# u's rows ordered by step and chunk, turned by VectorE; state tables loaded by GpSimd, a block at a time

## The chip, the cores and the metric
The kernel runs on one core of a Trainium2 chip. The metric is the device time of one execution in microseconds, median of the runs.

## The reference
A trunk of two decoder layers on 256 tokens of width 2048, in float32. Layer 0 mixes tokens by a chunked gMLP unit, layer 1 by an S5 state space. Each layer then has a SwiGLU block (width 5632) and a gated per-layer embedding; a last RMS norm follows. The part that the change touches:

```
x = x + sigmoid(rms_norm(x) @ ple_w_gate[0]) * (p[0] @ ple_w_proj[0])   # stage gate0
u = rms_norm(x) @ w_in                                                   # stage win
bu = B_bar u            (128 groups of 16 channels, complex state of 64)
s[t] = lam_bar * s[t-1] + bu[t]                                          # scan over 256 tokens
y = Re(C s) + D u;  g = gelu(y);  val, gate = split(g @ w_out)           # stage out1
x = x + val * sigmoid(gate)
```

The recurrence is computed in 32 chunks of 8 steps: a table TQ takes a chunk's 8 steps of u to the increment of the state, a scan over 32 chunks gives the state at each chunk's start, TD takes it to the 8 outputs, and TK adds what the steps of a chunk give each other.

## The kernel before, in words
Every large product goes through one pipeline of 792 weight tiles (two blocks of 128 rows by 512 columns, 512 KB). SP loads tile t into RAW, ACT writes its rounded part WHI (L771), VectorE the rest WLO (L1049), and TensorE (PE) multiplies: 12 matmuls a tile (L1515 to L1517). The ring has four places, so ACT and VectorE run at most three tiles ahead of PE. `plan()` lists the tiles by stage: v, us, out0, up0a, dn0a, up0b, dn0b, gate0, win, out1 and so on; W0 is the first tile of win. Each engine has its list written out by hand: `until(t)` does that engine's part of the tiles up to t + 2, and what stands behind it is done between tiles, in order. A wait holds up everything behind it on that engine.

Operands are turned in two ways: the last four blocks of a stage by PE through `turn`, the others by a VectorE block transpose ZT, four stores to zd in DRAM (L485), and a load HT (L489); `high` (ACT) and `low` (VectorE) then write the operand's two parts, with a scale from VEC.

Tables. In the stages up0a to dn0b GpSimd computes, for each of 16 blocks, QT and DT; at BUILD_A PE transposes QT by eight 128x128 transposes (`turn_tables`, L1624) into two banks, ACT copies them to QS (L898), SP stores QS, DT and later EXP to tabq, tabd, tabk. At BUILD_B PE computes `taps` (L1633).

Use. In gate0 and win SP loads TQ, TE, TD, TK for a duo of two blocks at a time (a megabyte each but TE), between the weight loads. In win, column n of u is taken by ACT into Z (scaled by RC, the reciprocal of ROOT), turned by PE (`turn_u`, L1724), copied by VectorE with the steps in front (`u_chunks`, UC, L1404), stored to ud and loaded as UP by ACT's queue (`store_u`, `spread_u`, L950 and L958). PE does `into_states(d)` (L1739) for duos d = 2n and 2n + 1, VectorE `scan(d)` (L1414 to L1430), PE `out_of_states(d)` (L1757, L1765), ACT `take_y` (L966), VectorE `turn_y` (L1437), ACT `y_high` (L973), VectorE `y_low` (L1442). On PE turn_u and out_of_states use the same banks 6 and 7, so out_of_states waits for u_chunks of the column behind. The places are tile numbers in UT_AT, INTO_AT, OUT_AT, Y_AT.

Of the kernel before, what the change touches and what calls it, by code (L numbers as in the profile page):

```python
# [13 lines left out]
P = 128  # L14
# [162 lines left out]
DSET = [0, 1, 2, 0, 1, 0, 1, 0]  # L177

# [16 lines left out]
def trunk(nc, x, p, norm_mix, norm_ffn, norm_ple, norm_final, gm_w_in, gm_ln_g, gm_ln_b, gm_w_s, gm_b_s,  # L195
# [3 lines left out]
    with ctx:  # L199
# [37 lines left out]
        ROOT = place("ROOT", [P, 2])  # L237
        MS = place("MS", [P, 2])
# [57 lines left out]
        QS = f_view("QS", [P, QP, 2, P], 32)  # L296
# [21 lines left out]
        UC = place("UC", [P, QB, T, NC], at=pt_at)  # L318
        UP = [op_view(f"UP{i}", [P, QB, GB, NC], 24 + 4 * i) for i in range(2)]
# [17 lines left out]
        ud = nc.dram_tensor("ud", (NT, QB, P, T * NC), F32).ap()  # L337
# [53 lines left out]
        qt_done = sem("qt_done")  # L391
# [13 lines left out]
        ut_done = sem("ut_done")  # L405
        uc_ready = sem("uc_ready")
        ud_in = [sem(f"ud_in{h}") for h in range(2)]
        up_in = [sem(f"up_in{d}") for d in range(2)]
# [25 lines left out]
        def feature_major(bank, h):  # L434

            if bank is None:
                return HT[:, 2 * h:2 * h + 2, :]
            return PS[:, bank + h, :].rearrange("p (k t) -> p k t", t=TOK)

# [30 lines left out]
        def _(sp):  # L470
# [71 lines left out]
            for b in range(KB):  # L542
# [5 lines left out]
                sp.dma_start(tabq[b], QS[:, :, :, :].rearrange("p q r n -> p (q r n)")).then_inc(q_out, 16)  # L548
# [5 lines left out]

            def duo(table, d):
                return table[2 * d:2 * d + 2].rearrange("b p n -> p b n")

            def load_tq(d):
                if d >= 2:
                    sp.wait_ge(in_done, d - 1)  # L560
                sp.dma_start(TQ[d % 2][:, :, :, :, :].rearrange("p b q r n -> p b (q r n)"), duo(tabq, d)).then_inc(tq_in[d % 2], 16)

            def load_te(d):
                if d >= 2:
                    sp.wait_ge(sd_ready, d - 1)
                sp.dma_start(TE[d % 2][:, :, :, :].rearrange("p r q k -> p r (q k)"),
                             tabe.rearrange("r p n -> p r n")[:, :, DP * NC * d:DP * NC * (d + 1)]).then_inc(te_in[d % 2], 16)

            def load_td(d):
                if set_before(d) is not None:  # L570
                    sp.wait_ge(out_of, set_before(d) + 1)
                sp.dma_start(TD[DSET[d]][:, :, :, :, :].rearrange("p b q r n -> p b (q r n)"), duo(tabd, d)).then_inc(td_in[DSET[d]], 16)

            def load_tk(d):
                sp.dma_start(TKK[DSET[d]][:, :, :, :].rearrange("p b g n -> p (b g) n"),
                             tabk[2 * d:2 * d + 2].rearrange("b (g c) (j n) -> (c j) (b g) n", g=GB, j=T)).then_inc(td_in[DSET[d]], 16)

            g0 = start("gate0")
            loads_to(g0 + 10)
            sp.wait_ge(split_used, end("dn0b", NT - 1))  # L580
            sp.wait_ge(rot_out, 16 * 4)
            sp.wait_ge(q_out, 16 * KB)
            sp.wait_ge(d_out, 16 * KB)
            sp.wait_ge(k_out, 16 * KB)
            load_tq(0)
            loads_to(g0 + 12)
            load_te(0)
            loads_to(g0 + 14)
            load_td(0)
            loads_to(g0 + 18)  # L590
            load_tk(0)
            loads_to(g0 + 21)
            load_tq(1)
            loads_to(g0 + 23)
            load_te(1)
            loads_to(g0 + 26)
            load_td(1)
            loads_to(g0 + 29)
            load_tk(1)
            loads_to(W0 + 9)  # L600
            sp.wait_ge(split_used, W0)
            load_td(2)
            loads_to(W0 + 12)
            load_tk(2)

            for g in range(13, 62):
                loads_to(W0 + g)
                for d in range(2, DUOS):
                    if g == INTO_AT[d - 2] - W0 + 9:
                        load_tq(d)  # L610
                    if g == INTO_AT[d - 2] - W0 + 12 + d % 2:
                        load_te(d)
                for d in range(3, DUOS):
                    if g == OUT_AT[set_before(d)] - W0 + 9:
                        load_td(d)
                    if g == OUT_AT[set_before(d)] - W0 + 10:
                        load_tk(d)
# [15 lines left out]
        def _(pool):  # L633
# [57 lines left out]
            for b in range(KB):  # L691
# [13 lines left out]
                if b:  # L705
                    pool.wait_ge(qt_done, b)
                else:
                    pool.wait_ge(mixed, NT)
# [30 lines left out]

            pool.wait_ge(split_used, end("dn0b", NT - 1))  # L740
# [4 lines left out]
            for d in range(DUOS):  # L745
                if d >= 2:
                    pool.wait_ge(rt_used, d - 1)
                decay(d)
# [10 lines left out]
        def _(act):  # L759
# [1085 lines left out]
```

## Time and profile before
| | us |
|---|---|
| median of 3 runs | 2298.37 (2298.2 to 2300.23) |
| the profiled execution's own time | 2298.6 |
| its span | 2296.8 |

| engine | busy us | share | instructions |
|---|---|---|---|
| PE | 2259.0 | 98% | 11514 |
| VectorE | 1420.2 | 62% | 1500 |
| ACT | 1037.0 | 45% | 1257 |
| GpSimd | 467.8 | 20% | 413 |

The span runs from the first instruction of the program to the last. PE's busy time is the union of its matmuls, whose ends are modelled. The DMA engines were busy for three quarters of the span with weights.

### The profile page before, as it was taken

The numbers are of one execution on the slowest core, as the hardware profiler recorded it, in microseconds if no ns is written. First come the engines' busy times: TensorE is split into PE (matmuls) and PEld (weight loads), VectorE is DVE, ScalarE is ACT, GpSimd is POOL, SyncE is SP. The second block draws the span as 40 slices with busy tenths as digits, with TensorE's granted clock in tenths as the row PEclk, the third lists the DMA queues.
The fourth block names the chain that finished last, engine by engine and source line by source line (L and its number), as shares of the span: only waits on it lengthen the run. The fifth ranks groups of instructions, "written<-read, shape, count | busy, mean of one in ns | idle before, by whom it ended". The sixth has DMA issues, their size and how long they took to land.

```text
span 2296.8 us, 28716 instructions
## 1 busy us (share of the span) xinstructions
PE 2259.0 (98%) x11514; PEld 1860.9 (81%) x11514; DVE 1420.2 (62%) x1500; ACT 1037.0 (45%) x1257; POOL 467.8 (20%) x413
## 2 busy tenths in 40 slices
PE   8999999999999999999998999999999999999998
PEld 7888888888888888888787788888888888888886
DVE  6877667666665766666676756555555445555665
ACT  5544454444444445444443345544444344444444
POOL 1245325456665544300000000000000000000001
PEclk9999999999999999999999999999999999999999
DMA  7667778777777787787969866667776566767764
GB/s 274 191 196 232 225 247 246 245 238 249 242 245 215 245 259 240 248 251 239 296 221 307 289 212 209 217 212 208 229 218 212 193 192 211 230 211 228 233 208 145
DMA packets 463942, 528.97 MB, mean 230 GB/s; under 512 B 219088, under 2 KB 244064, under 8 KB 463296
## 3 DMA queue, kind: packets, MB, share of 16 engines
q1 hardware_dynamic: 444160, 518.90, 71.8%
q10 hardware_dynamic: 18880, 4.74, 0.9%
q0 software_dynamic: 768, 3.48, 0.4%
q8 instruction: 91, 1.49, 0.3%
q14 instruction: 43, 0.35, 0.0%
HBM read 474.62 MB, written 52.43 MB: 229 GB/s over the span
## 4 chain that ended last, share of the span: by engine, by line
PE 88%; DVE 6%; DMA 4%; issue 1%; ACT 1%; SPq 0%; ACTq 0%; DVEq 0%
PE PS L1515 28%; PE PS L1516 28%; PE PS L1517 28%; DVE WLO L1049 2%; DMA HT<-zd 2%; DMA RAW<-in_gm_w_in 1%; PE PS L1624 1%; DMA ud<-UC 0%; ACT WHI L771 0%; PE PS L1633 0%; DVE Z L1312 0%; PE PS L1821 0%; PE PS L1822 0%; PE PS L1823 0%; PE PS L1765 0%
## 5 line engine op out<-in xcount | busy, mean ns | idle before, releaser
L1049 DVE TENSOR_TENSOR WLO<-RAW,WHI 128x1024 fp32r<-128x1024 f32 x783 | 1034.0, 1332 | 714.8 <-ACT WHI L771 710.8
L771 ACT ACTIVATE WHI<-RAW 128x1024 fp32r<-128x1024 f32 x783 | 825.1, 1060 | 899.1 <-PE PS L1517 796.5
L1515 PE MATMUL PS<-WHI,OP 128*128 128x512 f32 x3104 | 1217.2, 392 | 9.5 <-DVE WLO L1049 9.4
L1516 PE MATMUL PS<-WLO,OP 128*128 128x512 f32 x3104 | 1209.5, 390 | 0.0
L1517 PE MATMUL PS<-WHI,OP 128*128 128x512 f32 x3104 | 1209.2, 390 | 0.0
L1515 PEld LDWEIGHTS PS<-WHI,OP 128*128 128x128 f32 x3104 | 583.2, 188 | 137.1 <-DVE WLO L1049 11.8
L1517 PEld LDWEIGHTS PS<-WHI,OP 128*128 128x128 f32 x3104 | 583.0, 188 | 122.2
L1516 PEld LDWEIGHTS PS<-WLO,OP 128*128 128x128 f32 x3104 | 583.4, 188 | 118.7
L755 POOL TENSOR_TENSOR ON<-X,GF 128x1024 f32<-128x1024 f32 x3 | 9.9, 3304 | 980.9 <-DVE X L1367 980.9
L695 POOL TENSOR_TENSOR TA<-BRAW,FAC 128x64 f32<-128x64 f32 x16 | 6.7, 421 | 338.4 <-DMA BRAW<-in_s_b_im 338.4
L1061 DVE TENSOR_TENSOR OP<-HT,OP 128x512 fp32r<-128x512 f32 x50 | 33.0, 702 | 64.8 <-ACT OP L785 64.8
L785 ACT ACTIVATE OP<-HT 128x512 fp32r<-128x512 f32 x50 | 28.8, 624 | 82.3 <-DMA HT<-zd 82.3
L737 POOL COPY RT<-RHO 128x248 f32<-128x248 f32 x8 | 6.2, 786 | 229.6 <-DVE CB L1421 229.6
L808 ACT ACTIVATE S<-PS,RC 128x512 f32<-128x512 f32 x66 | 41.6, 682 | 23.2 <-PE PS L1517 23.1
L1067 DVE SCALAR_TENSOR_TENSOR OP<-HT,VEC,OP 128x256 fp32r<-128x256 f32 x60 | 25.2, 482 | 32.4 <-ACT OP L790 32.4
L790 ACT ACTIVATE OP<-HT,VEC 128x256 fp32r<-128x256 f32 x60 | 25.6, 498 | 37.2 <-DMA HT<-zd 37.2
L732 POOL TENSOR_TENSOR DT<-TA,TB 128x512 f32<-128x512 f32 x16 | 33.9, 2116 | 1.3
L1098 DVE BATCH_NORM_STATS2 STAT<-X 128x6 f32<-128x512 f32 x54 | 34.0, 670 | 0.0
L1354 DVE SCALAR_TENSOR_TENSOR Z<-PS,RC,S 128x512 f32<-128x512 f32 x44 | 30.9, 742 | 4.7 <-PE PS L1517 4.4
L905 ACT ACTIVATE EXPF<-PS 128x128 f32<-128x128 f32 (+7 forms) x128 | 17.8, 267 | 35.0 <-PE PS L1633 35.0
L898 ACT ACTIVATE QS<-PS 128x1024 f32<-128x1024 f32 x16 | 16.4, 1024 | 34.0 <-PE PS L1624 34.0
L1086 DVE STREAM_TRANSPOSE ZT<-Z 128x1024 f32<-128x1024 f32 x25 | 31.1, 1245 | 0.9
(216 smaller groups left out, 1072.6 us busy)
## 6 DMA issues: line engine op xcount, KB each, us to landing
RAW<-in_ffn_w SPq DMA_DIRECT2D x528, 512.0 KB, 4.5
RAW<-in_gm_w_in SPq DMA_DIRECT2D x64, 512.0 KB, 4.6
RAW<-in_ple_w_gate SPq DMA_DIRECT2D x64, 512.0 KB, 4.7
RAW<-in_s_w_out SPq DMA_DIRECT2D x64, 512.0 KB, 4.6
zd<-ZT SPq DMA_DIRECT2D x160, 128.0 KB, 3.1
HT<-zd SPq DMA_DIRECT2D x40, 512.0 KB, 6.6
RAW<-in_gm_w_out SPq DMA_DIRECT2D x32, 512.0 KB, 4.9
RAW<-in_s_w_in SPq DMA_DIRECT2D x32, 512.0 KB, 6.0
```

Source lines behind the costliest of these rows:

```text
L732: G_.tensor_tensor(DT[:, :, 1, :, :], TA[:, :, :, :], TB[:, :, :, :], ALU.subtract).then_inc(d_ready, 1)
L771: A_.activation(hi_of(t), RAW[:, t % RING, :], ACT.Copy).then_inc(hi_ready, 1)
L785: A_.activation(OP[:, block_ + 2 * h:block_ + 2 * h + 2, 0:TOK], feature_major(bank, h), ACT.Copy).then_inc(operand_hi, 1)
L808: last = A_.activation(dst(th), acc(stage, n)[:, th, :], func, scale=RC[:, RMS[stage], th:th + 1])
L1049: V_.tensor_tensor(lo_of(t), RAW[:, t % RING, :], hi_of(t).bitcast(F32), ALU.subtract).then_inc(lo_ready, 1)
L1061: V_.tensor_tensor(OP[:, blocks, TOK:2 * TOK], feature_major(bank, h), OP[:, blocks, 0:TOK].bitcast(F32), ALU.subtract).then_inc(operand_r ...
L1086: V_.transpose(ZT[:, :, :, :].rearrange("p h f a -> p (h f a)"), Z[:, :, :].rearrange("p h n -> p (h n)")).then_inc(zt_ready, 1)
L1098: last = V_.bn_stats(STAT[:, th, 6 * n:6 * n + 6], src[:, th, NW * n:NW * n + NW])
L1354: last = V_.scalar_tensor_tensor(Z[:, th, :], acc(stage, n)[:, th, :], RC[:, i_rms, th:th + 1], S[:, th, :], ALU.mult, ALU.mult)
L1515: T_.matmul(dst[:, th, :], hi, WHI[:, slot, f], start=begin, stop=False)
L1516: T_.matmul(dst[:, th, :], hi, WLO[:, slot, f], start=False, stop=False)
L1517: last = T_.matmul(dst[:, th, :], lo, WHI[:, slot, f], start=False, stop=finish)
```

## The change
- In gate0's four operands (`high`, `low`) the tokens are reordered, steps first and then chunks, so that win's product u has its rows by step and chunk.
- RC for win must be in that order: GpSimd stores ROOT to rootd and loads it as ROOTU (`turn_root`), and VectorE takes the reciprocal of ROOTU.
- `turn_u` is now one VectorE block transpose of Z to UT; UC, u_chunks and PE's transposes of Z are gone. ud has one column's worth in one store, and UP is loaded by four DMAs of 32 partitions with rows of 2 KB; PE's operand slices follow.
- `turn_tables` is now one VectorE block transpose of QT to QS; PE's transposes and ACT's copy are gone; SP stores QS by four DMAs.
- TQ, TD, TK (a block at a time) and TE are issued by GpSimd at places in TQ_AT and so on; SP issues weights alone there.
- OUT_AT is one tile later for six duos, and so is Y_AT.

```diff
-UT_AT = [W0 + 8 * n + 8 for n in range(NT)]
+U_AT = [W0 + 8 * n + 9 for n in range(NT)]
 INTO_AT = [W0 + 8 * (d // 2) + 14 + d % 2 for d in range(DUOS)]
-OUT_AT = [W0 + 8 * (d // 2) + 17 + 2 * (d % 2) for d in range(DUOS - 2)] + [W0 + 42, W0 + 43]
+OUT_AT = [W0 + 8 * (d // 2) + 18 + 2 * (d % 2) for d in range(DUOS - 2)] + [W0 + 42, W0 + 43]
+ROOT_AT = W0 + 3
+TQ_AT = [(G0 + 1, G0 + 3), (G0 + 13, G0 + 15)]
+TD_AT = [(G0 + 5, G0 + 7), (G0 + 18, G0 + 20), (W0, W0 + 2)]
+TK_AT = [(G0 + 9, G0 + 11), (G0 + 22, G0 + 24), (W0 + 4, W0 + 6)]
+TE_AT = [G0 + 12, G0 + 26]
+TQ_AT += [(W0 + g, W0 + g + 1) for g in (15, 17, 23, 25, 31, 33)]
+TD_AT += [(W0 + g, W0 + g + 1) for g in (19, 27, 29, 35, 37)]
+TK_AT += [(W0 + g, W0 + g + 1) for g in (21, 29, 31, 37, 39)]
+TE_AT += [W0 + g for g in (18, 19, 26, 27, 34, 35)]
...
-                sp.dma_start(tabq[b], QS[:, :, :, :].rearrange("p q r n -> p (q r n)")).then_inc(q_out, 16)
+                for pb in range(4):
+                    sp.dma_start(tabq[b].rearrange("(c j) (q s a) -> j q c s a", c=4, s=4, a=32)[:, :, :, pb, :],
+                                 QS[32 * pb:32 * pb + 32, :, :, :]).then_inc(q_out, 16)
...
+            def turn_root():
+                pool.wait_ge(root_ready, RMS["win"] + 1)
+                for h in range(2):
+                    pool.dma_start(rootd[h].unsqueeze(1), ROOT[:, h:h + 1]).then_inc(root_out, 16)
+                pool.wait_ge(root_out, 32)
+                for h in range(2):
+                    pool.dma_start(ROOTU[:, h:h + 1], rootd.rearrange("a (k h i) -> h i (a k)", h=2, i=T // 2)[h],
+                                   allow_slow_non_contiguous=True).then_inc(root_in, 16)
...
+            for t in range(G0, TK_AT[DUOS - 1][1] + 1):
+                pool.wait_ge(split_used, t)
+                for d in range(DUOS):
+                    for bl in range(2):
+                        if t == TQ_AT[d][bl]:
+                            load_tq(d, bl)
+                        if t == TD_AT[d][bl]:
+                            load_td(d, bl)
+                        if t == TK_AT[d][bl]:
+                            load_tk(d, bl)
+                    if t == TE_AT[d]:
+                        load_te(d)
+                if t == ROOT_AT:
+                    turn_root()
...
             def store_u(n):
-                for h in range(2):
-                    act.wait_ge(uc_ready, 2 * n + h + 1)
-                    act.dma_start(ud[n, 2 * h:2 * h + 2].rearrange("m p n -> p m n"),
-                                  UC[:, 2 * h:2 * h + 2, :, :].rearrange("p m j k -> p m (j k)")).then_inc(ud_in[h], 16)
+                act.wait_ge(ut_ready, n + 1)
+                if n:
+                    act.wait_ge(up_in, 64 * n)
+                act.dma_start(ud[:, :], UT[:, :, :, :].rearrange("p h f k -> p (h f k)")).then_inc(ud_in, 16)
 
             def spread_u(n):
+                act.wait_ge(ud_in, 16 * (n + 1))
                 if n >= 2:
                     act.wait_ge(out_of, 2 * n - 2)
...
+                for i in range(4):
+                    act.dma_start(UP[n % 2][i:P:4, :, :, :, :].rearrange("p g m q k -> p g (m q k)"),
+                                  ud.rearrange("(i g c) (h n) -> i (c h) g n", g=2, c=CH, h=2)[i]).then_inc(up_in, 16)
...
-                    if W0 + g == UT_AT[n] + 2:
+                    if W0 + g == U_AT[n] + 1:
                         store_u(n)
-                    if W0 + g == UT_AT[n] + 4:
+                    if W0 + g == U_AT[n] + 2:
                         spread_u(n)
...
+            def turn_tables(b):
+                until(BUILD_A[b] + 1)
+                dve.wait_ge(q_ready, b + 1)
+                if b:
+                    dve.wait_ge(q_out, 64 * b)
+                V_.transpose(QS[:, :, :, :].rearrange("p q c a -> p (q c a)"),
+                             QT[:, :, :, :, :].rearrange("p q r c j -> p (q r c j)")).then_inc(qs_ready, 1)
...
+            def turn_u(n):
+                dve.wait_ge(act_took, ACT_COUNT["win", n])
+                if n:
+                    dve.wait_ge(up_in, 64 * n)
+                V_.transpose(UT[:, :, :, :].rearrange("p h f k -> p (h f k)"), Z[:, :, :].rearrange("p h n -> p (h n)")).then_inc(ut_ready, 1)
...
+            until(W0 + 7)
+            dve.wait_ge(root_in, 32)
+            V_.reciprocal(RC[:, RMS["win"], :], ROOTU[:, :]).then_inc(rc_ready, 1)
...
             def out_of_states(d):
-                pe.wait_ge(uc_ready, 2 * min(n + 2, NT))
```

## Rows read from the trace of the kernel before

**Rows 1.** Windows: length; busy us (instructions) of PE, PEld, DVE, ACT, POOL; PEclk; DMA share; GB/s.
```profile
208.80:1094.00 885.20, 885.20 (x4284) 727.65 (x4285) 563.50 (x489) 403.22 (x548) 374.87 (x310) 1.00 0.78 243
...
1207.30:1214.00 6.70, 5.36 (x100) 4.34 (x101) 2.32 (x3) 2.72 (x4) 0.00 (x0) 0.50 0.78 242
```

**Rows 2.** Time line of PE in gate0: start, us, what, [idle before, releaser].
```profile
1099.08 0.50 PE L1515 MATMUL PS<-WHI,OP 128*128 128x512 f32 x1 [2.94 <-DVE WLO L1049]
...
1126.50 0.50 PE L1515 MATMUL PS<-WHI,OP 128*128 128x512 f32 x1 [2.45 <-DVE WLO L1049]
```

**Rows 3.** Groups of PE by form: count, busy us, mean ns, idle before, releaser.
```profile
L1624 PE MATMUL PS<-IDENT,QT 128*128 128x128 f32 x128 | 16.6, 272 | 0.0
...
L1757 PE MATMUL PS<-TK,UP 128*32 128x128 f32 x256 | 10.3, 312 | 11.8 <-DVE UC L1404 11.8
```

**Rows 4.** Time line of PE's weight loads around a table's transposes.
```profile
324.13 0.19 PEld L1517 LDWEIGHTS PS<-WHI,OP 128*128 128x128 f32 x1
324.35 1.03 PEld L1624 LDWEIGHTS PS<-IDENT,QT 128*128 128x128 f32 x8
325.35 0.19 PEld L1515 LDWEIGHTS PS<-WHI,OP 128*128 128x128 f32 x1
```

**Rows 5.** Groups of ACT and VectorE, columns as in rows 3.
```profile
L771 ACT ACTIVATE WHI<-RAW 128x1024 fp32r<-128x1024 f32 x783 | 825.1, 1060 | 899.1 <-PE PS L1517 796.5 <-DMA RAW<-in_gm_w_in 31.6 <-DMA RAW<-in_ffn_w 25.9
L973 ACT ACTIVATE OP<-YG 128x512 fp32r<-128x512 f32 x8 | 9.2, 1149 | 16.5 <-DVE YG L1437 16.5
...
L1086 DVE STREAM_TRANSPOSE ZT<-Z 128x1024 f32<-128x1024 f32 x25 | 31.1, 1245 | 0.9
L1442 DVE TENSOR_TENSOR OP<-YG,OP 128x512 fp32r<-128x512 f32 x8 | 8.8, 1096 | 0.0
L1437 DVE STREAM_TRANSPOSE YG<-YP 128x512 f32<-128x512 f32 x8 | 5.6, 705 | 0.1
```

**Rows 6.** Time line of SP's queue in gate0: start, us that its issues took.
```profile
1076.50 3.41 SPq L485 DMA_DIRECT2D zd<-ZT  x4
...
1082.20 5.59 SPq L478 DMA_DIRECT2D RAW<-in_ple_w_gate  x2
```

**Rows 7.** The chain that ended last, in order of time: start, us, what.
```profile
1087.83 7.26 DMA HT<-zd
...
1112.46 10.05 DMA HT<-zd
...
1246.53 10.28 DMA ud<-UC
1256.83 2.28 ACTq L958
```

**Rows 8.** Time line of VectorE in win.
```profile
1193.48 0.69 DVE L1414 TENSOR_TENSOR CA<-PS,TE 128x512 f32<-128x512 f32 x1 [2.41 <-PE PS L1739]
...
1206.06 1.23 DVE L1049 TENSOR_TENSOR WLO<-RAW,WHI 128x1024 fp32r<-128x1024 f32 x1
...
1231.49 0.69 DVE L1414 TENSOR_TENSOR CA<-PS,TE 128x512 f32<-128x512 f32 x1 [0.70 <-PE PS L1739]
...
1306.57 0.69 DVE L1414 TENSOR_TENSOR CA<-PS,TE 128x512 f32<-128x512 f32 x1 [0.59 <-PE PS L1739]
```

**Rows 9.** DMA issues: queue, count, KB each, median us from issue to landing.
```profile
tabq<-QS SPq DMA_DIRECT2D x16, 512.0 KB, 5.3
...
BRAW<-in_s_b_re SPq DMA_DIRECT2D x16, 32.0 KB, 3.6
...
AN<-in_s_a_re POOLq DMA_DIRECT2D x1, 32.0 KB, 5.5
```

**Rows 10.** Time line of ACT in win.
```profile
1207.92 1.05 ACTq L950 DMA_DIRECT2D ud<-UC  x2
1209.01 1.28 ACT L966 ACT_TABLE_LOAD   x1 [6.60 <-DVE UC L1404]
1212.57 1.08 ACT L966 ACTIVATE YP<-PS 128x256 f32<-128x256 f32 x2 [2.28 <-PE PS L1765]
```

More of the change, by code:

```diff
@@ L177 @@
 DSET = [0, 1, 2, 0, 1, 0, 1, 0]
+G0 = start("gate0")
+ROOT_AT = W0 + 3
[7 more added lines that the diff above has]
+TE_AT += [W0 + g for g in (18, 19, 26, 27, 34, 35)]
 def set_before(d):
@@ L237, in trunk @@
         ROOT = place("ROOT", [P, 2])
+        ROOTU = place("ROOTU", [P, 2])
         MS = place("MS", [P, 2])
@@ L578, in _ @@
[L578 to L592, printed above, removed]
@@ L777, in high @@
             def high(q):
-                _, n, _, block_, row, _, bank = QUADS[q]
+                stage, n, _, block_, row, _, bank = QUADS[q]
                 for h in range(2):
@@ L789, in high @@
                             k = 4 * QUADS[q][2] + 2 * h + m
-                            last = A_.activation(OP[:, block_ + 2 * h + m, 0:TOK], feature_major(bank, h)[:, m, :],
-                                                 ACT.Identity, scale=VEC[:, row, k:k + 1])
+                            high_, whole = OP[:, block_ + 2 * h + m, 0:TOK], feature_major(bank, h)[:, m, :]
+                            if stage == "gate0":
+                                high_, whole = by_steps(high_), of_tokens(whole)
+                            last = A_.activation(high_, whole, ACT.Identity, scale=VEC[:, row, k:k + 1])
                         last.then_inc(operand_hi, 1)
@@ L1055, in low @@
             def low(q):
-                _, n, _, block_, row, _, bank = QUADS[q]
+                stage, n, _, block_, row, _, bank = QUADS[q]
                 for h in range(2):
@@ L1066, in low @@
                             b = block_ + 2 * h + m
-                            last = V_.scalar_tensor_tensor(OP[:, b, TOK:2 * TOK], feature_major(bank, h)[:, m, :],
-                                                           VEC[:, row, k:k + 1], OP[:, b, 0:TOK].bitcast(F32),
-                                                           ALU.mult, ALU.subtract)
+                            low_, whole, high_ = OP[:, b, TOK:2 * TOK], feature_major(bank, h)[:, m, :], OP[:, b, 0:TOK].bitcast(F32)
+                            if stage == "gate0":
+                                low_, whole, high_ = by_steps(low_), of_tokens(whole), by_steps(high_)
+                            last = V_.scalar_tensor_tensor(low_, whole, VEC[:, row, k:k + 1], high_, ALU.mult, ALU.subtract)
                         last.then_inc(operand_ready, 1)
@@ L1371, in gated, with gates @@
                 stats(c, X)
-            def gates(stage, i):
+            def gates(stage):
                 for n in range(NT):
@@ L1378, in gates @@
                 moments()
-                until(end(stage, NT - 1) + 7)
-                reciprocal(i)
+            def turn_tables(b):
[5 more added lines that the diff above has]
+                             QT[:, :, :, :, :].rearrange("p q r c j -> p (q r c j)")).then_inc(qs_ready, 1)
             def own(b):
+                turn_tables(b)
                 until(BUILD_B[b] + 2)
@@ L1450, in _ @@
                 for n in range(NT):
-                    if W0 + g == UT_AT[n] + 1:
-                        u_chunks(n)
+                    if W0 + g == U_AT[n]:
+                        turn_u(n)
                 for d in range(DUOS):
@@ L1781, in _ @@
                     turn(AFTER[t])
-                for m in range(NT):
-                    if t == UT_AT[m]:
-                        turn_u(m)
                 for d in range(DUOS):
```

145 lines of the change are left out of this document (45 added, 100 removed).

## The prediction
> **What bounds the kernel now.** I read the windows first (busy time and granted clock by stretch), then PE's time line and groups for its idle time, then the chain of waits and the time lines of the engines that end it. PE is the bound: from 208.8 to 1094 us, the start of out0 to that of gate0, where the tables are built, it is busy 885.20 of 885.20 us, while VectorE is busy 563.50 of them [rows 1]. The reader is to see that every PE instruction taken out there is time gained, and that VectorE has room. It then idles in two places. In the stage gate0 it waits 2.94 and 2.45 us for WLO [rows 2]. In the stage win it waits before out_of_states: 11.8 us in three waits, released by u_chunks' copy UC [rows 3]. The clock is granted at 0.50, the 1.2 GHz level, from 1207.3 to 1214.0 [rows 1]: the first of these waits ends inside that stretch, when VectorE is through with the copy behind the WLO of 1206.06 [rows 8].
>
> **Tables.** Of each of the 16 tables PE loses its eight transposes (L1624, x128) [rows 3]. Weight loads start at 324.13 and 324.35 (0.22 apart), and the tile's next at 325.35 [rows 4]: 1.00 where 0.22 is usual, so some 0.79 lost per table, 16 x 0.79 = 12.7 us. ACT loses 16 copies QS. VectorE gains 16 transposes of 128x1024; the same operation as L1086, 1.245 us [rows 5], 19.9 us in all beside 321.7 us of its idle time [rows 1]. It stands right behind a WLO section, three tiles ahead of PE; what is queued behind it is the next WLO, needed 8 us later. If that cover were gone it would cost up to 19.9. SP's one store of a table becomes four of 128-byte pieces. The nearest row is a foursome of zd stores in the same pieces, 3.41 us of SP's time [rows 6]; one goes out in each pair of up columns already, without a wait on PE [rows 1], and the ring of four weight tiles hides it, so I take 0. Unhidden, three more issues of 0.85 us each would be 16 x 2.6 = 41 us; below nothing it can't be, since nothing is taken from SP there. Sum so far: -12.7.
>
> **gate0.** Both waits have one chain: ACT stands at high() until HT has landed, WHI and WLO stand behind it. HT was issued at 1087.83 and took 7.26 us, and at 1112.46 with 10.05 us [rows 7]. Ahead of the first, SP was held 5.59 us over two weight issues, right behind the table load TK [rows 6]. The change takes TQ, TE, TD and TK out of SP's queue. The first HT can then be issued about 5 us earlier, as soon as zd has landed; 2.94 us are needed, so all of that wait goes. The second was behind a megabyte of TD and four weights; the TK blocks of GpSimd now lie beside it on the same DMA engines, so I count 1.5 of 2.45. What is late next is PE's own pace. -4.4 us (bounds: 0, and 5.4, both waits). The rearranged operands of these four quads read with a step of eight elements; the nearest row is y_high, L973, with a stepped read of 512 elements in 1149 ns [rows 5], half of that for 256: 0.57 us, under the idle time of ACT and VectorE. I take 0; bounds 0 and 1.
>
> The Trainium skill speaks against this term: DMA: Bandwidth & Descriptors, section "Issuing engines are not separate DMA queues", says that transfers issued by any engine run on the same 16 DMA engines and interleave, so that spreading issues saves only the sequencer's time, usually small. By it gate0 would gain little and the sum would be 4.4 us higher. What this trace has against "small" is the 5.59 us; which of both holds is my first rival.
>
> **win.** Here the removed waits (11.8 us), the four turns of u on PE (4 x 0.79, L1724) and the clock at half are not simply gained, because the order on ACT and VectorE makes a new loop. VectorE does scan(2k), a WLO, scan(2k+1), a WLO, then turn_u(k+1) in place of u_chunks: scan(0) starts at 1193.48, the second WLO ends at 1207.29, 13.8 us [rows 8]; the next instruction overlaps it by 0.1, so 13.7. turn_u takes 1.25 [rows 5]. Only then can ACT store u. Spread_u now stands one tile behind store_u and in the same pass of ACT's list ahead of take_y(2k). So ACT, in order, waits for the landing of ud, issues four spreads, and only then empties the bank that out_of_states(2k+1) on PE waits for (yp_ready). Queued behind on ACT are WHI, and so WLO.
> - Landing of ud: 512 KB in rows of 4 KB. Nearest: tabq's store, the same size and rows, 5.3 us [rows 9]. Far end: ud today, 10.28 us at 1246.53 [rows 7], beside a megabyte of TQ. I take 5.5, since TQ now goes earlier.
> - Four issues: ACT's two issues of ud take 1.05 [rows 10], so 2.1 for four; far end 2.28 for one, the second half's spread today [rows 7], with 2048 pieces where a new one has 64.
> - take_y 1.08 [rows 10].
> - From take_y(2k)'s end to scan(2k+2): WHI, WLO, turn_y, y_high, WHI, take_y, WHI, WLO, turn_y, y_high, WHI, WLO, y_low = 4 x 1.06 + 3 x 1.23 + 2 x 0.71 + 2 x 1.15 + 1.10 + 1.08 = 13.8 us [rows 5, 8, 10].
>
> A round, from one even scan to the next, is 13.7 + 1.25 + 5.5 + 2.1 + 1.1 + 13.8 = 37.5 us. Today's two rounds run from 1231.49 to 1306.57 [rows 8], 37.5 each, with a half clock in one. PE's own work in a round is 8 tiles of 12 x 0.227 and four state products of 2.1 each (an estimate: today's round less tiles, waits and half clock): some 30 us. It idles 4 us in front of each odd out_of_states and 1 to 3 us in front of WLO. A half clock behind such a wait (it takes 3.4 us of work) falls into this idle time and no longer counts. The first round also has the Gelu table load, 1.28 us [rows 10], which out_of_states(0) hides today: 13.7 + 1.25 + 5.5 + 2.1 + 1.3 + 1.1 + 13.8 = 38.7 against 38.0 from 1193.48 to 1231.49 [rows 8]: +0.7. So -0.1 for two rounds, +0.7 for the first. Ahead of it, -0.8 for the first turn of u, and a new wait: RC of win comes by two DMA legs over GpSimd. ACT takes the root at tile 5 of the stage and needs RC at tile 8, 8.2 us later; a leg is 1.2 us of issues and a landing between 3.6 (BRAW, 32 KB, from SP) and 5.5 us (AN, from GpSimd, in a full queue) [rows 9], two legs 9.6 to 13.4: late by 1.4 to 5.2. VectorE waits there with WLO queued behind it, with three tiles in hand, and spread_u had 2 us in hand; I take +0.8, bounds 0 and +4. Behind the last round PE is ahead of VectorE rather than behind it: -1. Stage: -0.4.
>
> Tables by GpSimd: 36 blocks and six TE in win. The closest to its use is the last TK, four tiles and a state product ahead, 13 us, against 5.3 to 5.5 us of landing [rows 9]: 0. If GpSimd stood behind a wait for longer than the 7 us between, PE would wait for the rest.
>
> **Sum.** Against the profiled execution's own 2298.6 us (span 2296.8): -12.7 - 4.4 - 0.4 = 2281.1; the median of the runs is 0.2 lower, so **2281 us**.
>
> **Rivals.**
> - A, gate0 stays as it is: GpSimd's blocks take the bandwidth that SP's did, HT lands as late as now. For it: the second HT took 10.05 us to land once issued, which is bandwidth. Against: the first stood behind 5.59 us of SP's own time. Time: 2281 + 4.4 = 2285.
> - B, ACT is held for less: ud lands in 4.5 and the issues take 1.5. Each microsecond is worth 3 (three rounds): -1.6 x 3 = 2276. For it: queue beside it is emptier; against: tabq's 5.3.
> - C, the other side: **ACT's hold behind ud** is as long as today's worst rows. The hold is 7.6 us in my sum (5.5 + 2.1). Each microsecond more costs three rounds and, past 1.5, the first spread too. At 10.3 of landing and 1.15 an issue the hold is 14.9, 7.3 more: 3 x 7.3 + 5.8 = +28, 2309. It decides from 4.7 us more, a hold of 12.3: 3 x 4.7 + 3.2 = 17.3 = 2298.4 - 2281. For it: the 10.28 and the 2.28. Against: those were rows of 1 KB and pieces of 128 bytes, with TQ issued just ahead.
> - D, the loads by GpSimd come late (a wait in its list, root's legs included): +4 to +12, some 2288. The Trainium skill has a mechanism for it: SBUF — State Buffer, section "SBUF: two separate sides", has GpSimd unable to write descriptors while VectorE runs a two-port copy. No run here shows it; VectorE's stage has WLO, scans and transposes, and its copies UC are taken out.
>
> **Chances.** Forecast 0.55, A 0.15, B 0.12, D 0.09, C 0.09. Range 2273 to 2293: below, B with all of gate0 and the tail; above, A with D's smaller half and a microsecond more of hold; C's 0.09 and the rest stay out. Less than 0.2% (4.6 us) is what a measurement of this kernel can't tell from none: faster by more than that has 0.88, within 0.02, slower 0.10.
>
> **What would show it.** Right: no L1624 row; out_of_states idle before d = 1, 3, 5, 4 us each, released by ACT YP, and none by VectorE before d = 0, 2, 4; scan(2) to scan(6) 75 us apart; ACT idle some 5 us before its spread issues; gate0's waits under 1 us. Wrong: PE waits on VectorE in the table stages; waits on TQ, TD or TK; odd waits over 6 us (C) or absent (the loop isn't there, and the time would be near 2270).

## The result and the profile after

The changed kernel takes 2307.23 us (median of 15 runs, 2300.82 to 2311.86), the kernel before, on the same chip, 2300.03 us (15 runs, 2297.56 to 2301.86). The ratio is 1.0029 with a 95% interval of 1.0020 to 1.0037: a little slower, by 7 us, where 17 us less had been forecast and 2273 to 2293 us given as the range.

The profiled execution of the changed kernel lies 5 us under that median: its own time is 2302.59 us, its span 2299.5 against 2296.8. I set the two traces side by side by the start of each weight tile's first matmul on PE. How much the difference grows over a stretch is what the stretch lost (plus) or won (minus). A stretch runs from the start of the tile ahead of it to the start of its last tile, so a wait in front of a tile counts with that tile. The last column has the same reading of the experiments' profiles (below), wherever a run left that stretch's code as it is in the changed kernel.

| stretch (tiles) | forecast us | measured us | with the same code, all such profiles |
|---|---|---|---|
| start to up0a (0 to 96) | 0 | +0.6 | -0.5 to +1.9 |
| 16 tables on PE (97 to 326) | -12.7 | -14.4 | -14.4 to -14.2 |
| end of dn0b, behind the last table (327 to 341) | 0 | +5.0 | +2.6 to +5.0 (8 profiles) |
| gate0 (342 to 397) | -4.4 | +7.9 | +7.7 to +11.2 (7) |
| first turn of u (398 to 405) | -0.8 | -0.7 | -0.8 to -0.7 |
| RC of win (406 to 408) | +0.8 | +5.9 | +4.9 to +12.2 (6) |
| the loop of win (409 to 440) | -0.4 | -1.5 | -1.6 to +6.0 (7) |
| sum | -17.5 | +2.8 | |

The tables and the first turn of u came out as forecast, the loop in this profile too. Three terms were wrong by 5 to 12 us each. One profile is one execution: in gate0, at RC and in the loop the same code differs by 3 to 8 us from one profile to the next, so a gain of a few microseconds in one of these stretches is only as sure as that. The first term, in the windows (columns as in [rows 1]) and the group of the new operation:

```profile
208.80:1094.00 885.20, 876.72 (x4170) 717.79 (x4169) 578.09 (x511) 393.77 (x541) 370.28 (x320) 1.00 0.83 246
```
```profile
L1393 DVE STREAM_TRANSPOSE QS<-QT 128x1024 f32<-128x1024 f32 x16 | 19.8, 1239 | 0.0
```

L1624 is gone and the transpose costs 1.24 us, hidden, as [rows 5] had it. But in a stretch in which PE was never idle [rows 1] it now is for 8.5 us (3.3 in the first two waits, the rest in gate0, which now begins inside this window). Its time line (start, us, what, idle before) shows where, and what is behind it:

```profile
978.86 0.47 PE L1532 MATMUL PS<-WHI,OP 128*128 128x512 f32 x1 [2.68 <-DVE WLO L1056]
...
1083.54 0.50 PE L1532 MATMUL PS<-WHI,OP 128*128 128x512 f32 x1 [1.27 <-DVE WLO L1056]
...
1093.24 0.79 PE L1532 MATMUL PS<-WHI,OP 128*128 128x512 f32 x1 [3.94 <-DVE WLO L1056]
...
1123.69 0.79 PE L1532 MATMUL PS<-WHI,OP 128*128 128x512 f32 x1 [3.75 <-DVE WLO L1056]
...
1178.92 0.79 PE L1532 MATMUL PS<-WHI,OP 128*128 128x512 f32 x1 [2.86 <-DVE WLO L1056]
...
1222.65 1.25 PE L1750 MATMUL PS<-TK,UP 128*32 128x128 f32 x17 [3.93 <-ACT YP L973]
...
1261.03 1.29 PE L1750 MATMUL PS<-TK,UP 128*32 128x128 f32 x20 [5.92 <-ACT YP L973]
...
1298.11 1.93 PE L1750 MATMUL PS<-TK,UP 128*32 128x128 f32 x32 [3.56 <-ACT YP L973]
```

The second and third from the top answer to the first of [rows 2], the fourth to its second. The 0.79 us where 0.50 stood is the half clock. From 965 to 1325 us, a granted clock of 0.50, the 1.2 GHz level, stands beside or behind such waits at seven places of the changed kernel, at two of the one before. One of them as a window:

```profile
1178.20:1185.00 6.80, 6.08 (x14) 4.79 (x15) 5.17 (x5) 3.79 (x5) 0.00 (x0) 0.50 0.96 312
```

The last three lines are the forecast's loop: no wait before out_of_states of an even duo, released by UC as in [rows 3], but one before each odd duo, released by YP, 3.6 to 5.9 us long. ACT's time line shows its hold (it waits, in order, until ud has landed, and only then issues the four loads of UP and empties the bank into YP):

```profile
1212.56 0.33 ACTq L957 DMA_DIRECT2D ud<-UT  x1
1213.00 1.06 ACT L780 ACTIVATE WHI<-RAW 128x1024 fp32r<-128x1024 f32 x1 [6.32 <-DVE UT L1419]
1217.61 2.54 ACTq L965 DMA_DIRECT2D UP<-ud  x4
1220.18 1.28 ACT L973 ACT_TABLE_LOAD   x1 [6.12 <-issue]
1221.47 1.03 ACT L973 ACTIVATE YP<-PS 128x256 f32<-128x256 f32 x2
```

The end of dn0b is SP's queue (start, us of the issues). Behind the last table's four stores stand the four of zd, and each foursome holds SP for 3 to 4 us longer than the 3.41 of [rows 6]; HT, which ACT waits for, goes out at 965.96 and lands at 974.77:

```profile
946.21 7.29 SPq L571 DMA_DIRECT2D tabq<-QS  x4
...
955.77 6.72 SPq L507 DMA_DIRECT2D zd<-ZT  x4
...
965.96 0.89 SPq L511 DMA_DIRECT2D HT<-zd  x1
```

In gate0 the chain of waits shows zd and HT, now beside GpSimd's table loads; 5.70 us of SP's time for the foursome where 3.41 stood [rows 6], HT 9.21 us where 7.26 stood [rows 7]. From HT's landing (1088.02) to the WLO that PE waits for it is 5.2 us, where it was 4.0:

```profile
1073.06 5.73 DMA zd<-ZT
...
1078.81 9.21 DMA HT<-zd
```
```profile
L802 ACT ACTIVATE OP<-HT,VEC 128x256 fp32r<-128x256 f32 x60 | 28.8, 551 | 45.0 <-DMA HT<-zd 45.0
```

(L802 was 498 ns on average, with 12 of the 60 changed.) And the root's two legs, in the chain of waits and on VectorE:

```profile
1164.81 8.73 DMA rootd<-ROOT
...
1174.54 3.02 DMA ROOTU<-rootd
```
```profile
1177.57 0.17 DVE L1464 RECIPROCAL RC<-ROOTU 128x2 f32<-128x2 f32 x1 [9.98 <-DMA ROOTU<-rootd]
```

### The profile page after: what moved, and what is told of

Its sections match the earlier page's. It is cut to its first block, busy times and chain, and to the rows that moved or that the text cites. A ratio compares the mean times of both kernels' runs of the same rounds, so it can differ in the third digit from the quotient of the medians.

```text
span 2299.5 us, 28479 instructions
## 1 busy us (share of the span) xinstructions
PE 2253.5 (98%) x11354; PEld 1853.0 (81%) x11354; DVE 1433.2 (62%) x1512; ACT 1024.1 (45%) x1241; POOL 497.2 (22%) x473
## 4 chain that ended last, share of the span: by engine, by line
PE 86%; DMA 5%; DVE 5%; issue 2%; ACT 1%; SPq 1%; ACTq 0%; POOL 0%; DVEq 0%; POOLq 0%
PE PS L1532 28%; PE PS L1533 27%; PE PS L1534 27%; DMA HT<-zd 2%; DVE WLO L1056 1%; DMA RAW<-in_gm_w_in 1%; DMA ud<-UT 1%; ACT WHI L780 1%; DMA zd<-ZT 0%; SPq L507 0%; DMA rootd<-ROOT 0%; PE PS L1642 0%; PE PS L1812 0%; PE PS L1811 0%; PE PS L1813 0%
## 5 line engine op out<-in xcount | busy, mean ns | idle before, releaser
L1056 DVE TENSOR_TENSOR WLO<-RAW,WHI 128x1024 fp32r<-128x1024 f32 x783 | 1023.2, 1318 | 691.9 <-ACT WHI L780 687.9
L1532 PEld LDWEIGHTS PS<-WHI,OP 128*128 128x128 f32 x3104 | 585.4, 189 | 150.4 <-DVE WLO L1056 19.1
L1077 DVE SCALAR_TENSOR_TENSOR OP<-HT,VEC,OP 128x256 fp32r<-128x256 f32 x60 | 27.9, 523 | 42.0 <-ACT OP L802 41.9
L802 ACT ACTIVATE OP<-HT,VEC 128x256 fp32r<-128x256 f32 x60 | 28.8, 551 | 45.0 <-DMA HT<-zd 45.0
L691 POOL TENSOR_TENSOR TB<-CT,LAMA 128x512 f32<-128x512 f32 x16 | 30.8, 1928 | 0.0
L690 POOL TENSOR_TENSOR TA<-CT,LAMA 128x512 f32<-128x512 f32 x16 | 30.1, 1882 | 1.3
```

Source lines behind the costliest of these rows:

```text
L691: step(G_.tensor_tensor(TB[:, :, :, :], c(0), up(1), ALU.mult))
L1056: V_.tensor_tensor(lo_of(t), RAW[:, t % RING, :], hi_of(t).bitcast(F32), ALU.subtract).then_inc(lo_ready, 1)
L1532: T_.matmul(dst[:, th, :], hi, WHI[:, slot, f], start=begin, stop=False)
```

## The experiments

All but the fifth start from the changed kernel (2307.23 us). Each was timed beside the kernel before, and the ratio is to that. "Less than the changed kernel" sets medians of different batches side by side, in which the kernel before had 2298.62 to 2300.05 us, so a difference of 1 to 2 us there says nothing. Stretches and tiles are compared with the trace of the changed kernel.

**1. The four stores one a tile.**
```diff
-                loads_to(BUILD_A[b] + 10)
-                sp.wait_ge(qs_ready, b + 1)
                 for pb in range(4):
+                    loads_to(BUILD_A[b] + 7 + pb)
+                    sp.wait_ge(qs_ready, b + 1)
```


> The changed kernel with one edit: a table's four stores of QS go out one a tile (tiles 7 to 10 after its build) instead of four at tile 10. Theory: PE's waits at 969.8 and 976.2 us of the changed kernel (0.6 + 2.7 us and a half clock, +5.0 us over tiles 338 to 341) come from SP, held 4.9 us in the last table's stores and 4.7 us in the zd stores right behind them. Then both waits go and the time falls by 4 to 5 us, to about 2302 us (the changed kernel's median is 2307); the other stages stay. Rival: it is the bytes in 128-byte pieces and not where SP stands; the waits stay within a microsecond and the time is unchanged. Second rival: the spread stores hold SP by 0.6 to 1 us in each of 16 tables and PE waits there; the time rises.

Measured: 2306.67 us, ratio 1.0025 (1.0015 to 1.0034). The waits behind the last table are gone, tiles 338 to 341 win 5.1 us, and no table stage lost anything. SP's queue there:

```profile
943.91 0.58 SPq L571 DMA_DIRECT2D tabq<-QS  x1
...
951.43 4.67 SPq L507 DMA_DIRECT2D zd<-ZT  x4
```

The median fell by 0.6 only, where 4 to 5 had been expected: the place is shown, its price in the median is not. What stood against it in the profiled execution (2308.43 us) is elsewhere, with the same code: gate0 took 2.3 us and the loop 5.3 us more, and the wait at tile 406, 2.86 us in the changed kernel's profile, was 9.38. The root's store had taken not 8.73 but 16.87 us:

```profile
1160.04 16.87 DMA rootd<-ROOT
```
```profile
1180.12 0.17 DVE L1464 RECIPROCAL RC<-ROOTU 128x2 f32<-128x2 f32 x1 [16.50 <-DMA ROOTU<-rootd]
```

**2. The root's order by PE.**
```diff
-                    pool.dma_start(rootd[h].unsqueeze(1), ROOT[:, h:h + 1]).then_inc(root_out, 16)
...
+                for h in range(2):
+                    for k in range(2):
+                        last = T_.matmul(PS[:, 6, h:h + 1], PM[:, k, h, :], ROOT[:, k:k + 1], start=(k == 0), stop=(k == 1))
...
-            V_.reciprocal(RC[:, RMS["win"], :], ROOTU[:, :]).then_inc(rc_ready, 1)
+            V_.reciprocal(RC[:, RMS["win"], :], PS[:, 6, 0:2]).then_inc(rc_ready, 1)
```


> The changed kernel with one edit: RC of win is brought into u's row order by four matmuls of one column (a 0/1 matrix that GpSimd builds from IDENT at tile W0) instead of two DMA legs over rootd. Theory: PE's wait of 2.86 us at 1176.05 and the half clock of 6.83 us from 1178.2, +5.9 us over tiles 406 to 408, are the two legs (13.3 us, landing at 1177.55). They go, the matmuls cost some 0.5 us: 5 to 6 us less, some 2302 us. Rival: the wait is that of VectorE's place in its list (turn_u and the scans behind), and another wait comes up at the next place; less than 2 us gained.

Measured: 2302.06 us, ratio 1.0006 (0.9996 to 1.0015). PE has no wait between 1125 and 1215 us; tiles 406 and 407 win 5.6 us and nothing comes back at once. The medians differ by 5.2 us, as the theory has it, and the rival falls. In the profiled execution (2304.88 us) the three waits of the loop were longer, 5.11, 8.42 and 4.69 us: ud landed after 10.2 us before the second of them, where it took 6.7 in the changed kernel, and ACT's hold was 12.8 us.

**3. take_y(2k) ahead of spread_u.**
```diff
-                    if W0 + g == U_AT[n] + 2:
-                        spread_u(n)
...
                     if W0 + g == OUT_AT[d] + 1:
                         take_y(d)
+                for n in range(NT):
+                    if W0 + g == U_AT[n] + 2:
+                        spread_u(n)
```


> The changed kernel with one edit: in ACT's pass, take_y(2k) stands ahead of spread_u instead of behind it. Theory (the loop of the prediction): ACT's wait for the landing of ud no longer holds take_y(2k), so out_of_states(1), (3), (5) start without their waits of 3.93, 5.92 and 3.56 us, and the three half clocks behind them go; UP comes 1 to 2 us later, which into_states has in hand. PE is then held by its own work: 8 to 13 us less, 2295 to 2299 us. Rival: PE is held by the round of VectorE and ACT as a whole (37.5 us) and the wait only moves, to into_states or to WLO behind the next spread: less than 3 us gained.

Measured: 2299.49 us, ratio 0.9998 (0.9986 to 1.0009), 7.7 less than the changed kernel. The three waits are gone (tile 417, tiles 425 and 426, and tile 433 win 5.5, 8.6 and 4.9), but smaller ones come up, since ACT still stands at ud, now with WHI behind it:

```profile
1227.46 2.06 PE L1734 MATMUL PS<-UP,TQ 128*64 128x32 f32 x64 [1.56 <-issue]
...
1247.25 0.50 PE L1533 MATMUL PS<-WHI,OP 128*128 128x512 f32 x1 [1.90 <-DVE WLO L1057]
...
1276.34 0.47 PE L1533 MATMUL PS<-WHI,OP 128*128 128x512 f32 x1 [1.36 <-DVE WLO L1057]
```

That is between the theory (8 to 13 us) and its rival (under 3): the wait moved in part. The loop's stretch is 3.3 us shorter in this pair of profiles.

**4. gate0's operands in their old order** (the reordering is left out, so u's rows don't come in the order that the rest of the kernel expects).
```diff
-                            if stage == "gate0":
-                                high_, whole = by_steps(high_), of_tokens(whole)
```
(and the like in `low`)


> The changed kernel without the reordering of gate0's four operands (high and low read and write the tokens in their own order), so u's rows are not by step and chunk: this part is left out. Theory: an operand's high and low take 0.75 and 0.68 us a block instead of 0.50 and 0.48, and since WHI and WLO stand behind them this is 1.2 us of each of the two long waits of gate0 (3.94 and 3.75 us); with them back at the old length the waits fall by 1.2 each, and the half clocks behind them may go too: 2.5 to 5 us less, about 2304 us. Rival: the waits are set by the landing of HT (9.2 and 9.5 us) alone; less than 1 us gained.

Measured: 2305.65 us, ratio 1.0020 (1.0006 to 1.0033). Gate0 wins 3.6 us; L800, the same instruction, is back at 498 ns, and the two long waits are 2.68 and 2.44 us, 1.3 less each. The stepped operands that I had counted as 0 are worth some 3 to 4 of the 7.9 us that gate0 lost (+4.2 here, where the seven profiles with the stepped ones have +7.7 or more); the rest is elsewhere. The median is 1.6 lower, which can't be told from nothing; the profiled execution has a wait of 10.1 us at tile 406.

```profile
L800 ACT ACTIVATE OP<-HT,VEC 128x256 fp32r<-128x256 f32 x60 | 25.6, 498 | 42.2 <-DMA HT<-zd 42.2
```
```profile
1118.74 0.51 PE L1528 MATMUL PS<-WHI,OP 128*128 128x512 f32 x1 [2.44 <-DVE WLO L1054]
```

**5. The kernel before with the table part alone**, its stores one a tile.


> The kernel before with the table part alone: QT turned to QS by one VectorE block transpose, QS stored by four DMAs, here one a tile; PE's transposes and ACT's copies of QS are out, all else as before. Theory: the change's loss lies wholly in its other parts, and this one gives what the prediction's first term said: 16 x 0.79 = 12.7 us less, 2287 us, with the waits of gate0 and win as before. Rival: the change of pace in the table stages moves where the half clocks fall and the four stores cost at the last table; 2290 to 2293 us.

Measured: 2283.77 us, ratio 0.9931 (0.9916 to 0.9946), 16.3 less than before. The 16 tables give 14.4 us, 0.90 each: 0.79 at the build's tile and 0.11 besides. Against the kernel before, the profile has +1.0 up to up0a, -14.4 in the tables, -0.7 from there to win (gate0's two long waits are 2.09 and 1.99 us) and -1.1 in win. The four stores, one a tile, cost nothing. So the change's first part is a gain once its stores are spread, and the loss is in those stores and in the other parts.

**6. GpSimd's first table loads away from zd and HT.**
```diff
-TQ_AT = [(G0 + 1, G0 + 3), (G0 + 13, G0 + 15)]
-TD_AT = [(G0 + 5, G0 + 7), (G0 + 18, G0 + 20), (W0, W0 + 2)]
-TK_AT = [(G0 + 9, G0 + 11), (G0 + 22, G0 + 24), (W0 + 4, W0 + 6)]
-TE_AT = [G0 + 12, G0 + 26]
+TQ_AT = [(G0 + 1, G0 + 2), (G0 + 18, G0 + 19)]
+TD_AT = [(G0 + 4, G0 + 5), (G0 + 27, G0 + 28), (W0 + 5, W0 + 7)]
+TK_AT = [(G0 + 7, G0 + 8), (W0 + 1, W0 + 3), (W0 + 9, W0 + 11)]
+TE_AT = [G0 + 10, G0 + 20]
```


> The changed kernel with one edit: GpSimd's loads of the first three duos' tables are moved out of the tiles in which gate0's columns go to zd and come back as HT (to tiles 1 to 10, 18 to 20, 27, 28 of gate0 and 1 to 11 of win). Theory: on the shared DMA engines they hold back the zd stores and HT (HT lands after 9.2 and 9.5 us, a zd store holds SP for 3.6 and 3.1 us); with them elsewhere HT lands 2 to 3 us sooner, gate0's waits (1.3 + 3.9 and 0.2 + 3.8 us) fall to those of the kernel before or under, and the time by 4 to 7 us, about 2302 us. Rival: HT is held back by the weights and its own 128-byte pieces; HT's landing changes by less than 1 us and the time by less than 2 us. A third: root's legs are held back by the loads now beside them, and the wait at tile 406 grows.

Measured: 2299.40 us, ratio 0.9996 (0.9986 to 1.0005), 7.8 less than the changed kernel; gate0 alone wins 8.8 us. The first HT is issued 5.2 us earlier (4.1 against PE's place) and lands 0.9 us quicker; the zd store held SP 1.13 us at its third issue, not 3.62:

```profile
1068.29 1.13 SPq L507
...
1069.46 4.13 DMA zd<-ZT
...
1073.61 8.30 DMA HT<-zd
```
```profile
1087.31 0.50 PE L1532 MATMUL PS<-WHI,OP 128*128 128x512 f32 x1 [0.72 <-DVE WLO L1056]
```

So the theory holds more by when HT can be issued than by its flight. Of the third theory: the wait at tile 406 was 8.8 us here, but it was 9.4 and 10.1 in two runs with the loads in their old place, so that is not shown.

**7. ROOT stored in 512-byte pieces.**
```diff
+                G_.tensor_copy(ROOTW[:, :, 0:1], ROOT[:, :].unsqueeze(2)).then_inc(wide_ready, 1)
...
-                    pool.dma_start(rootd[h].unsqueeze(1), ROOT[:, h:h + 1]).then_inc(root_out, 16)
+                    pool.dma_start(rootd[P * h:P * h + P, :], ROOTW[:, h, :]).then_inc(root_out, 16)
```


> The changed kernel with one edit: ROOT goes to rootd in pieces of 512 bytes a partition (its value and 127 fillers) instead of 4 bytes; it comes back in 4-byte reads as before. In the runs so far the store of 2 x 512 bytes took 8.7 to 17 us to land, and the weights issued beside it 8 to 16 us, where 5 is usual. Theory: it is the 4-byte writes to DRAM that hold up the DMA engines; then the stores land in 4 to 6 us, weights beside them in 5 to 6, VectorE's wait for ROOTU ends 3 to 10 us sooner, PE's wait at tile 406 (2.9 to 10.1 us in four profiles) is under 2 us, and the time falls by 4 to 9 us. Rival: it is GpSimd's queue and the legs one behind the other that cost; landings and the wait stay as they are.

Measured: 2297.89 us, ratio 0.9992 (0.9983 to 1.0001), 9.3 less than the changed kernel. Stores with 128 times the bytes land in 3.5 and 5.2 us; VectorE waits 5.41 us and PE not at all at tile 406:

```profile
1170.74 0.17 DVE L1471 RECIPROCAL RC<-ROOTU 128x2 f32<-128x2 f32 x1 [5.41 <-DMA ROOTU<-rootd]
```

The DMA view of 1160 to 1176 us (issues, KB each, median us to landing), first of run 1, with 4-byte pieces, then of this one:

```profile
RAW<-in_s_w_in SPq DMA_DIRECT2D x3, 512.0 KB, 15.1
rootd<-ROOT POOLq DMA_DIRECT2D x2, 0.5 KB, 13.0
```
```profile
RAW<-in_s_w_in SPq DMA_DIRECT2D x5, 512.0 KB, 4.6
TK<-tabk POOLq DMA_DIRECT2D x2, 512.0 KB, 5.5
...
rootd<-ROOTW POOLq DMA_DIRECT2D x2, 64.0 KB, 4.3
```

In those 16 us all DMAs together moved 1.47 MB in run 1 and 3.62 MB here.

**8. Four edits together**: the stores one a tile, the root by PE, the loads moved, and u's store and spread issued by GpSimd, with turn_u ahead of scan of the odd duo.
```diff
-U_AT = [W0 + 8 * n + 9 for n in range(NT)]
+U_AT = [W0 + 8 * n + 8 for n in range(NT)]
...
+                for n in range(NT):
+                    if t == U_AT[n]:
+                        store_u(n)
+                    if t == U_AT[n] + 1:
+                        spread_u(n)
```
(in GpSimd's list; out of ACT's)


> The changed kernel with four edits together: stores of QS one a tile, the root's order by four matmuls, the table loads moved as in the run of that alone, and u's store and spread issued by GpSimd instead of ACT, with turn_u one tile earlier, ahead of scan of the odd duo. Theory: ACT no longer waits for ud, so the loop of the prediction is gone; PE waits in win are under 2 us in all; from the changed kernel's 2307: -5 (last table), -5 to -10 (root), -4 (gate0), -8 to -12 (win): 2279 to 2285 us. Rival: GpSimd, in order, holds its table loads behind the wait for ud, so out_of_states or into_states waits for TK or TQ; 2290 us or more.

Measured: **2265.85 us**, ratio 0.9852 (0.9838 to 0.9867), 34 less than the kernel before and better than the theory by 13. From tile 409 on win is 17.9 us shorter than in the changed kernel. Neither state product waits (one WLO wait of 1.18 us is left in win), and the clock never falls in win:

```profile
L1742 PE MATMUL PS<-UP,TQ 128*64 128x32 f32 x512 | 16.5, 223 | 0.0
...
L1759 PE MATMUL PS<-TK,UP 128*32 128x128 f32 x256 | 8.6, 276 | 0.0
```

L1750, the same group in the changed kernel, had 11.2 us busy and 13.4 idle ahead of it.

**9. u by GpSimd, without the other three edits** (it still has two parts: GpSimd issues u's store and spread, and turn_u stands one tile earlier).


> The changed kernel with one edit: GpSimd issues u's store and spread, not ACT, and turn_u stands one tile earlier, ahead of scan of the odd duo. Theory: this alone is what took 20 us out of win in the kernel with four edits (two of out_of_states' waits of 3.9 and 5.9 us and one of 3.6 with the half clocks behind them: -5.5, -7.7, -4.9 us at tiles 417, 425, 433, less what returned behind each); no wait over 1.5 us before out_of_states or into_states, 14 to 18 us less than the changed kernel, 2289 to 2293 us. Rival: the loop also needed the earlier root; then some waits come back and the gain is under 10 us.

Measured: 2283.51 us, ratio 0.9924 (0.9899 to 0.9949), 23.7 less than the changed kernel. The three waits are gone, and nothing comes back; from tile 409 on 19.1 us are won, although the root's wait was 7.83 us. The theory holds, the rival falls. The gain was larger than the 14 to 18 us expected (four runs, 2277.57 to 2288.64).

**10. Run 8 with turn_u behind the scan again.**


> The kernel with four edits, but turn_u behind scan of the odd duo as in the changed kernel (one tile later). It tells which half of the fourth edit works. Theory: the engine that waits for ud is what matters, and the place of turn_u only sets when UP lands: UP is 6 to 7 us later, which is more than into_states(2), (4), (6) have in hand, so PE waits 1 to 3 us for UP in front of each and the time is 2269 to 2275 us. Rival: UP has the time in hand, no wait appears: 2266 us.

Measured: 2270.45 us, ratio 0.9872 (0.9857 to 0.9887), 4.6 over run 8. Four waits of 0.6 to 2.1 us stand before into_states:

```profile
L1742 PE MATMUL PS<-UP,TQ 128*64 128x32 f32 x512 | 16.5, 223 | 4.3 <-issue 3.7 <-DMA UP<-ud 0.6
```

So the place of turn_u is worth some 4 us (4.6 in the medians, 3.4 in the stretch), and the rest of the fourth edit's gain, some 15 us, goes with the engine that waits for ud.

**11. Run 8 with the tables loaded later still.**


> The kernel with four edits and the tables of the second and third duo loaded later still (TQ at tiles 27, 28 of gate0, TD and TK in tiles 2 to 11 of win), so that no table is in flight with the second zd store and HT. Theory: the last long wait of gate0 (2.8 us at 1108.7 and a half clock) goes: 2 to 3 us less, about 2263 us. Rival: HT's 8 us are those of its own pieces and the weights, the wait stays; and the denser loads in win's first tiles make PE wait for RAW there: 2266 to 2270 us.

Measured: 2264.91 us, ratio 0.9851 (0.9836 to 0.9866): not told apart from run 8. The wait of 2.79 us went to 0.63, and one of 2.46 came up at the third HT, now beside two TQ blocks.

**12. ROOT stored in 4-byte pieces by ACT's queue.**
```diff
-                    pool.dma_start(rootd[h].unsqueeze(1), ROOT[:, h:h + 1]).then_inc(root_out, 16)
...
+                act.dma_start(rootd[h].unsqueeze(1), ROOT[:, h:h + 1]).then_inc(root_out, 16)
```


> The changed kernel with one edit: the same two stores of ROOT to rootd in 4-byte pieces are issued by ACT instead of GpSimd; ROOTU is loaded by GpSimd as before. With 512-byte pieces from GpSimd the stores landed after 3.5 and 5.2 us. Theory: the size of the pieces alone makes the stall; then it stays: the stores land after 8 to 17 us, weights beside them after 8 to 16, 2305 to 2309 us. Rival: it takes both the 4-byte pieces and GpSimd's queue; then the stores land in 2 to 5 us, the weights in 5 to 6, and the time is that of the run with 512-byte pieces, 2298 us.

Measured: 2306.96 us, ratio 1.0033 (1.0021 to 1.0046). The stores landed after 5.6 and 8.3 us, three weights beside them after 11 to 12, PE waited 5.40 us. The stall stays with either of the two queues; GpSimd's is not its cause.

```profile
RAW<-in_s_w_in SPq DMA_DIRECT2D x4, 512.0 KB, 11.7
...
rootd<-ROOT ACTq DMA_DIRECT2D x2, 0.5 KB, 7.0
```

## Why the prediction was wrong

- **Tables, PE: right.** -12.7 forecast, -14.4 measured: 0.79 at each build as read from [rows 4], and 0.11 more that those three lines didn't show.
- **Tables, the four stores: wrong.** The step was "one goes out in each pair of up columns already ... so I take 0". That holds for 15 tables. The sixteenth stands next to zd's foursome in the same queue, and then SP is held in both: +5.0 us here, 2.6 to 4.2 in seven other profiles. My nearest row was one foursome alone; two in a row is what I should have looked for in SP's list. Run 1 takes it away.
- **gate0: wrong, and with the wrong sign.** The step was "the first HT can then be issued about 5 us earlier ... all of that wait goes". SP was freed of TK (5.59 us, [rows 6]) but was then held in the zd stores themselves and in the weights, as the DMA engines were as full as before (busy for 0.96 of the time from 1068 to 1088.5 us, 1.00 in the stretch that answers to it before). HT went out 2.0 us earlier against PE's place (4.7 us ahead of tile 377, not 2.7) and took 2.0 us longer. Rival A stopped at no gain and took the bandwidth for a draw; run 6, in which nothing but the places of the loads differs, is 8.8 us better in gate0. The other part is the stepped operands: "under the idle time of ACT and VectorE. I take 0" forgot that WHI and WLO stand behind these very instructions when PE is already waiting: 1.3 us in each long wait, 3.6 in all (run 4). And the two long waits, longer now, are each followed by a half clock, which they were not before.
- **win, the loop: the mechanism right, the size by some luck.** 4 us in front of each odd out_of_states was forecast, 3.93, 5.92 and 3.56 came, released by YP; scan(2) to scan(6) took 75.4 us for 75; the stretch is -1.5 against -0.4. ud landed in 4.8 to 6.7 us and four spreads took 2.6 (5.5 and 2.1 taken). But six other profiles with the same loop have ud landing in 4.3 to 10.2 us, odd waits of 3.4 to 8.4 us and a stretch of -1.6 to +6.0, above +1.5 in five of the six. The waits of 1 to 3 us in front of WLO, in which a half clock was to vanish, did not come; a half clock stands beside each odd wait. The loop's price was seen and set against the old waits, and the sum of both was near nothing; run 9 says what the order in ACT's and VectorE's lists cost: 19 us.
- **RC of win: mis-sized.** The mechanism was named (late by 1.4 to 5.2 us, three tiles in hand). In the changed kernel's profile the two legs took 13.3 us, at the end of the forecast's 9.6 to 13.4, the first 9.3 of it. What was priced too low there is the wait that follows: +0.8 with bounds of 0 and +4, where 2.86 us of waiting and the half clock behind it made +5.9. In four of the six profiles with these legs the landing was mis-sized too: it was taken from transfers of 32 KB, up to 5.5 us, where the second of the 0.5 KB stores took 15.4 to 17.1 us and both legs 19 to 21. PE's wait at tile 406 was 2.86, 9.38, 3.11, 10.14, 8.81 and 7.83 us in the six. That can explain in part why the profiled execution lies 5 us under the median, and why 15 runs spread by 11 us where the kernel before has 4 and run 5 has 3. It is not shown: which execution had which wait is known for the profiled ones alone, run 2, without the legs, spreads by 8 us, and run 1, with them, by 6.

Rival D (late loads by GpSimd, the root's legs included, 2288 us) had the legs' place and about their price, and none of the rest; the reason given for it from the Trainium skill, VectorE in GpSimd's way, was not the one: GpSimd issued the stores 0.5 us after ROOT was there, and run 12 has the stall without it. Rival B, a shorter hold of ACT, did not occur. Rival C's did in single rounds: the hold was 7.4 to 9.2 us in the changed kernel's profile, but 12.8 in the second loop round of run 2, over the 12.3 from which C was to decide, and that round took 41.9 us. The rule of the Trainium skill that was weighed against gate0, DMA: Bandwidth & Descriptors, section "Issuing engines are not separate DMA queues", had more right than my row: moving the issues to GpSimd won nothing there, and run 6 shows that what was in flight together on the common DMA engines decided.

Partly settled: why the second 4-byte store took 9 us in some executions and 15 to 17 in others. In the two profiles with 9 us (the changed kernel, run 3) SP had issued a weight 0.2 to 0.5 us ahead of the first store; in the four with 15 to 17 us (runs 1, 4, 6 and 9) it issued one 0.3 to 0.5 us behind it. The six agree, but no run varies this order by itself.

## What to carry to other kernels

A transfer that is moved to another engine's queue still meets the old ones on the DMA engines: read from the time line what is in flight at its new place, above all beside a chain of store, landing and load that an engine waits for. Let no engine that feeds the critical one wait in order for a DMA's landing; of the 19 us that the order of win's lists cost here, some 15 went with that, and on the idle GpSimd the same wait cost nothing. A few hundred bytes aren't a small transfer if they are stored in 4-byte pieces side by side; with one column a partition, reorder on an engine or pad the pieces. And where one stretch of the same code differs by 3 to 8 us between profiles, read it in several before you price an edit there.

## What the runs showed of the hardware

Two stores of 128 pieces of 4 bytes to DRAM held up the traffic beside them. In run 1 three weight transfers issued beside them, 512 KB each in 2 KB pieces, took 12.1, 16.3 and 15.1 us; the DMA view of 1160 to 1176 us has 92 GB/s there, and 226 GB/s with 512-byte pieces in run 7. By the trace, 39 packets of 2 KB began between 1163 and 1168 us in run 1, and took 1.2 to 2.4 us on average from one microsecond to the next, 0.085 when undisturbed; 640 began in the same stretch of run 7. ROOTU's 4-byte reads from DRAM landed in 2.1 to 3.6 us in runs 1, 3 and 7; in run 12, where three weights were still held up, they took 5.7 and 7.1.

The Trainium skill, DMA: Bandwidth & Descriptors, section "Specifications", says that transfers below 512 bytes make the engine read, modify and write. That agrees in kind with the pair of runs 1 and 7; but in the changed kernel the 128-byte packets of tabq's stores took 0.013 us each at 949 to 951 us, and the 2 KB packets that began in the same two microseconds 0.087 on average, near the 0.085 of undisturbed ones. These too are under that size, so being under it does not by itself make the stall. Run 7 changed two things at once: the pieces are longer, and they lie 512 bytes apart in DRAM where the 4-byte pieces lay side by side. Which of the two ends the stall no run here separates.

Stores in small pieces can also hold the engine that issues them: the third of four stores in 128-byte pieces took SP 4.94 us at 947.84 us and 4.68 us at 957.10 in the changed kernel, where the other three of a foursome took 0.6 to 1.0.
